# Spreading a bias copy over eight paced pieces, moving two weight loads, and adding a dummy square root in a one-core decoder layer

## What is computed

```python
h = rmsnorm(x, norm1_g[l])
cols = split_columns(h @ w_in[l])               # q, kc, vc, ks, vs, kw, vw, gates, c_q, c_kv, k_rope
o_nsa = nsa_mixer(..., t5_bias)                 # logits get t5_bias[t5_bucket(distance)]
o_mla = mla_mixer(c_q, c_kv, k_rope, positions, q_norm_g, w_q_up, kv_norm_g, w_kv_up)
x = x + concat(rmsnorm(o_nsa), rmsnorm(o_mla)) @ w_out[l]
x = x + peer_ffn(rmsnorm(x, norm2_g[l]), ...)
return rmsnorm(x, final_g)
```

## Time and profile before

| what | value |
|---|---|
| time, median of 3 runs | 1681.74 us (1678.98 to 1685.91) |
| the profiled execution | 1683.38 us, its span 1681.5 us |
| PE busy | 1614.3 us, 96% |
| DVE / ACT / POOL busy | 1311.4 / 661.5 / 358.1 us |
| mean granted clock of PE | 0.987 |
| chain that ended last | PE 51%, DVE 8%, DMA 8% |

### The profile page before, as it was taken

How to read it: one execution, slowest core, us unless ns; L and a number is a source line. 1 busy time by engine, 2 the same in 40 slices (tenths; PEclk the granted TensorE clock), 3 DMA queues, 4 the chain that set the end, 5 groups by cost and what they waited for, 6 DMA issues and landing times.

```text
span 1681.5 us, 25784 instructions
## 1 busy us (share of the span) xinstructions
PE 1614.3 (96%) x9131; PEld 1361.9 (81%) x9131; DVE 1311.4 (78%) x3054; ACT 661.5 (39%) x1037; POOL 358.1 (21%) x303
## 2 busy tenths in 40 slices
PE   7999999899999999998999999999999999999997
PEld 5877767788865678998999899997888887888885
DVE  3467777554668789998998888866888888888887
ACT  3345555432210233443544346653333333333333
POOL 1000020101000343232136550002222223222220
PEclk9999999999999999999999999999999999999999
DMA  7541000223236789887889995458999999999995
GB/s 256 165 139 37 2 2 2 83 84 125 75 94 226 227 299 311 281 286 260 266 275 348 343 331 193 127 158 292 315 324 332 320 321 342 326 318 326 318 331 203
DMA packets 198446, 380.78 MB, mean 226 GB/s; under 512 B 16291, under 2 KB 130787, under 8 KB 197708
## 3 DMA queue, kind: packets, MB, share of 16 engines
q1 hardware_dynamic: 159008, 226.39, 40.9%
q0 software_dynamic: 37952, 143.18, 24.4%
q10 hardware_dynamic: 1388, 9.98, 1.5%
HBM read 340.66 MB, written 41.98 MB: 228 GB/s over the span
## 4 chain that ended last, share of the span: by engine, by line
PE 51%; DVE 8%; DMA 8%; issue 2%; ACT 2%; SPq 0%; DVEq 0%; ACTq 0%
PE psum L2026 27%; PE psum L108 15%; PE psum L1775 7%; DMA v_first<-uT 4%; PE psum L1796 2%; DMA acts_in<-acts 2%; DMA u_raw<-uT 2%; DVE u_lo L1693 2%; DVE u_rows L1684 1%; ACT u_hi L1533 1%; DVE hot L1714 1%; DVE v_lo L1969 1%; DVE is L1708 1%; DVE x_back L1987 0%; DVE x_back L2016 0%
## 5 line engine op out<-in xcount | busy, mean ns | idle before, releaser
L108 PE MATMUL psum<-h_hi,u_hi 128*128 128x384 f32 x832 | 288.1, 346 | 19.8 <-DVE u_lo L1693 19.6
L2026 PE MATMUL psum<-v_hi,wa_hi 128*128 128x512 f32 x768 | 300.1, 391 | 6.3 <-DVE wa_lo L1976 4.4
L2026 PE MATMUL psum<-v_lo,wa_hi 128*128 128x512 f32 x768 | 299.6, 390 | 0.0
L2026 PE MATMUL psum<-v_hi,wa_lo 128*128 128x512 f32 x768 | 299.4, 390 | 0.0
L108 PE MATMUL psum<-h_lo,u_hi 128*128 128x384 f32 x832 | 280.7, 337 | 0.0
L108 PE MATMUL psum<-h_hi,u_lo 128*128 128x384 f32 x832 | 280.7, 337 | 0.0
L1524 POOL DMA_INDIRECT u_rows<-u,eid x128 | 190.8, 1490 | 342.4 <-DVE sdot L1684 301.6
L1937 ACT ACTIVATE v_hi<-v_raw 128x1024 fp32r<-128x1024 f32 x126 | 133.7, 1061 | 320.0 <-PE psum L2026 237.5
L1917 POOL DMA_INDIRECT v_rows<-v,eid x128 | 133.5, 1043 | 503.5 <-DVE x_back L1987 367.7
L1969 DVE TENSOR_TENSOR v_lo<-v_raw,v_hi 128x1024 fp32r<-128x1024 f32 x126 | 154.3, 1225 | 42.3 <-ACT v_hi L1937 41.1
L108 PEld LDWEIGHTS psum<-h_hi,u_hi 128*128 128x128 f32 x832 | 158.1, 190 | 24.7 <-DVE u_lo L1693 24.4
(11 more groups left out here) (317 smaller groups left out, 2664.5 us busy)
## 6 DMA issues: line engine op xcount, KB each, us to landing
v_raw<-v SPq DMA_DIRECT2D x126, 512.0 KB
u_raw<-uT SPq DMA_DIRECT2D x66, 512.0 KB
v_first<-uT SPq DMA_DIRECT2D x62, 512.0 KB
acts<-act_out SPq DMA_DIRECT2D x128, 192.0 KB
acts_in<-acts SPq DMA_DIRECT2D x128, 192.0 KB
wq_raw<-wq SPq DMA_DIRECT2D x16, 512.0 KB, 3.6
gates<-dense ACTq DMA_DIRECT2D x4, 2048.0 KB, 11.1
gates<-gates SPq DMA_DIRECT2D x31, 256.0 KB
```

The costliest lines, as they stand in the source:

```text
L108: mm = pe.matmul(bank, w[:, k, :], x[:, k, :], start=(i == 0), stop=(i == n - 1))
L2026: mm = pe.matmul(psum[:, 2 * t + b, :], w[:, c, ts], v[:, c, bs], start=(first and n == 0), stop=(last and n == 2), skip_group_check=True)
```

## The change

1. The copy of 4096 KB from `bias_rows` to `bias_rep` becomes eight DMAs of 512 KB, one for each head. They are issued behind the first four `pairs` copies, two at each count of `tile_mm` from 3 to 6. POOL waits for all eight ahead of the skewed load.
2. ScalarE's two loads of the up weights go from ahead of the first split to behind its split of tile 8 (`UP_AT = C0`, which is 8).
3. In `combine`, ScalarE waits for `fg`, takes a dummy square root (of zero times a column of `fg`) into a place that is written again later, and waits for it, ahead of the last norm.

```diff
             pool.wait_ge(b_out, 16)
-            pool.dma_start(io.bias_rep.rearrange("p (h n) -> p h n", h=HEADS),
-                           io.bias_rows.partition_broadcast(P)).then_inc(b_rep, 16)
-            pool.wait_ge(b_rep, 16)
...
                     pool.dma_start(pairs[DH:P, c, g, 0:S - 1], src[:, 1:S]).then_inc(pair_ok, 16)
+                if c == 0:
+                    rep = io.bias_rep.rearrange("p (h n) -> p h n", h=HEADS)
+                    rows = io.bias_rows.partition_broadcast(P)
+                    for h in range(HEADS):
+                        pool.wait_ge(tile_mm, R0 + 3 + h // 2)
+                        pool.dma_start(rep[:, h:h + 1, :], rows[:, h:h + 1, :]).then_inc(b_rep, 16)
+            pool.wait_ge(b_rep, 16 * HEADS)
             pool.dma_start(m.bias[:, :, :], skew).then_inc(b_tile, 16)
...
-            act.dma_start(m.wq_up[:, :, :], io.wq_up).then_inc(up_in, 16)
-            act.dma_start(m.wkv_up[:, :], io.wkv_up).then_inc(up_in, 16)
             split(0)
...
             for i in range(2, C0 + 2):
                 split(i)
+                if i == UP_AT:
+                    act.dma_start(m.wq_up[:, :, :], io.wq_up).then_inc(up_in, 16)
+                    act.dma_start(m.wkv_up[:, :], io.wkv_up).then_inc(up_in, 16)
...
+            act.wait_ge(fg_in, 16)
+            act.activation(stat[:, 2, QT - 1:QT], fg[:, 0:1], ACT.Sqrt, scale=0.0).then_inc(f_warm, 1)
+            act.wait_ge(f_warm, 1)
             for i, t in enumerate(order):
                 act.wait_ge(f_add, i + 1)
```

More of the change, by code:

```diff
@@ L191, in project @@
         UP_BANKS = 6
+        UP_AT = C0
         def is_row(i):
@@ L1863, in combine @@
         rest_in, fg_in = sem("rest_in"), sem("fg_in")
+        f_warm = sem("f_warm")
         block = ctx.enter_context(nc.Block())
```

## The result

| | before | changed |
|---|---|---|
| median of 12 runs each, us | 1679.89 (1676.3 to 1689.28) | 1674.41 (1665.6 to 1686.41) |
| ratio, 95% interval | 1 | 0.9952 (0.9931 to 0.9974) |
| span of the profiled execution, us | 1681.5 | 1673.1 |

The change makes the kernel 0.48% faster (0.26% to 0.69%), some 8 us by the ratio (5.5 by the medians), and the interval excludes that nothing changed. 1674.41 is 2.0 us above the predicted 1672.4, within its range of 1668.5 to 1678. Part of this closeness is luck: the kernel before has a median of 1679.89 us over twelve runs, where the forecast started from the 1681.74 of three. 9.4 us off 1679.89 would be 1670.5, and the measurement is 3.9 above that. The gain is just short of the bound of 0.5%, on the other side of which I had put 0.52 of the chance.

What follows compares the result with a forecast made beforehand. TensorE, busy for 96% of the span, was taken as the bound, with time to win only at its idle or low-clock places. 1683.38 - 8.27 - 1.10 = 1674.0 us profiled, so 1672.4 as median; range 1668.5 to 1678.

Steps and rivals of the forecast that it cites:

- the bound of 0.5%: Whole kernel: smallest difference a measurement can tell from no change, 8.4 us, that is 1673.3 us; chance of faster 0.52.
- The stall (part 1): Row tile 2 on PE: start comes 5.41 us forward and full clock returns 2.86 us, sum 8.27 us.
- the turns: DMA engines at the start: queues alternate one for one, 32 KB of copy per 2.7 KB of load, 2.0 us a turn.
- The loads beside the pieces: Row-tile loads during the paced copy: land in 5.6 us, within a slack of 8.6 us, so no cost.
- The up weights (part 2): Start and behind the split of tile 8: moving the two loads gains nothing and costs nothing.
- The end (part 3): Last norm in `combine`: the dummy brings square root's table load forward, gaining 1.10 us.
- The sum: Whole kernel: 8.27 and 1.10 us off the profiled execution; median 1672.4 us, 9.4 us (0.56%) less; chance 0.66.
- A: PE's later idle stretches: a lower clock answers one, or the 2.86 us is not returned; 1675.3 us; chance 0.12.
- B: Last norm: the dummy gives between -0.4 and +0.85 us; 1672.7 to 1673.9 us; chance 0.12.
- C: Row tiles: pieces starve their loads, 10.4 us for each stall; 1682.8 us with one, 1693 with two; chance 0.05.
- D: Row tile 2: full DMA engines, not the copy's packets, slow the load, so it still waits; 1676.5 us; chance 0.05.
- E: Whole kernel: the run's own spread may put a median 2 us to either side; lies over all, no separate chance.

Runs made afterwards that it cites:

- e1: Kernel before with only the copy in eight paced pieces, up weights at the start, no dummy; 1679.17 us in one execution.
- e6: Changed kernel with the copy as one DMA of 4096 KB issued at `tile_mm` 3; 1676.76 us in one execution.
- e4: Kernel before with the copy in eight 512 KB pieces, all issued at once at the old place, no dummy; 1672.13 us in one execution.
- e7: Changed kernel with the up weights loaded behind the split of column tile 10; ratio to the kernel before 0.9938 over 12 runs.
- e5: Changed kernel with the paced pieces cut by partitions, each 16 partitions with 32 KB rows; 1672.48 us in one execution.
- e8: Kernel before with the copy in two 2048 KB DMAs at once, rows of 16 KB, no dummy; 1671.73 us in one execution.
- e9: Kernel before with the copy in eight pieces at once at the old place, plus the dummy square root; ratio 0.9931 over 9 runs.
- e2: Kernel before with only the up-weight loads moved behind the split of tile 8, one copy as before; 1684.18 us in one execution.

## Why the prediction was right, and where it was not

**The stall (part 1): right, 8.27 us forecast, 8.3 measured.** e1 has 41.2 - 32.9. Both terms, the idle time and the low clock, are borne out: PE's granted clock is 1.00 throughout the stage, and e6 has brought both back.

**Why the load was slow: the turns are right, the place of the pacing was left open.** The prediction had it that small rows make the turns short, and added that by the rule of the Trainium skill (DMA: Bandwidth & Descriptors, Queues, rings and completion order) 4 KB rows would come in turns of 9 to 17 and only the pacing would help. e4 has no pacing and no stall, with about one packet for one in the queues, so the trace doesn't agree with that rule. The prediction had called the rule refuted before, and its reason was not enough: the copy has only eight packets an engine, so by the rule the load would have waited behind all of them, which also gives some 16 us. Only the packet counts and e4 decide it. Its turn of 16.1 / 8 = 2.0 us was also too long: a large packet takes 1.35, and the rest of the 16.1 is mostly the wait for the first packet.

**The loads beside the pieces: a little short.** 5.6 us were forecast from the 8.3 us of the earlier trace rows, which was the longer of two such loads (the next one beside `bias` landed in 5.9). Tile 6 to 8's landed in 5.1, 5.7 and 6.6, and tile 9's, 512 KB, in 8.0. They grow from tile to tile, as the backlog does: 341 GB/s asked for, and 302 to 309 carried from 35 to 50 us. All are under the slack, so PE didn't wait for a split.

**The up weights (part 2): the step that failed, by 0.4 us.** "Cost nothing" rested on the slack of a row tile's load against PE. It left out that ScalarE and VectorE must also copy the row products behind the split of tile 9, in the same short time. Tile 9's load met the last pieces and then the up weights, and PE waited for VectorE. e1 and e7, each without the up loads there, are 0.4 us quicker. But e5 has them at the same place and lost nothing: there tile 9's load landed in 6.5 us. So the up loads cost something only on top of the late pieces, and 0.4 us is the reading of one execution.

**The end (part 3): right.** 1.10 us forecast; the step from scaling to reciprocal went from 1.52 to 0.42, and the tail is 11.6 to 11.7 us in the five kernels without the dummy and 10.6 to 10.7 in the five with it. The table load did not wait for the gain, as the prediction had read from the earlier trace rows. The Trainium skill (ScalarE: Activation LUTs, What ACT_TABLE_LOAD costs) has 2.66 us for the switch with its drain; by the tail it is worth 1.0, and the measurement decides.

**The sum.** 8.3 + 1.1 - 0.4 = 9.0 us, against 9.4 forecast and some 8 measured with an interval from 4.4 to 11.6 (0.26% and 0.69% of 1679.89). The two profiled spans differ by 8.4, but this is partly chance. Tile 1 started 1.1 us later in the one of the changed kernel, which leaves 6.8 us at tile 9 and still 6.8 at the start of `experts`; `experts` then took 7.6 us less and `combine` 7.0 more, in code that is the same; the tail is 1.0 shorter. By the traces' clock records PE was at the low level for 13.7 us of `experts` before and 6.8 after, and for 3.4 and 10.2 us of `combine`. At half speed that is at most 3.4 us of each difference (an estimate); the rest is not explained.

**The rivals.** A (the clock takes it back) didn't happen in the stage touched: the clock is 1.00 there in all the kernels without a stall of several us. From tile 9 to `experts` it is low for 13.7 us both before and after, and that stretch takes 413.8 us in both. Behind that, the low stretches differ from execution to execution, and no run shows whether the change moves them. B's worst case is excluded by the 1.04 us that the Square has left. C's slack was right (8.7 us in e6) and its price per tile wrong: the copy is over after one stall, so the next load has nothing to share with. One such stall gives back the stage of before (41.0 us in e6), so C could hardly have made the kernel slower. D's forecast, that tile 2 still waits, is refuted by the changed kernel and e1, and its reason by e4, where the engines are full (share 1.03) and tile 2 doesn't wait. E is what decided between faster and same. The forecast was 1 us beyond the bound and the measurement 0.3 short of it; a chance of 0.52 for one side of it was as much as could be said.

## What to carry to other kernels

Here a DRAM copy with rows of 32 KB, and to a lesser degree one of 16 KB, slowed the small loads that shared the DMA engines with it, since the packets went about one for one. To look for this elsewhere, count the load's packets on an engine, multiply by the time of one packet of the copy, add the wait for the first packet (some 4 us here) and about 1 us for the landing, and compare the sum with the load's slack. For the kernel before this sum gives 10.8 + 4 + 1 = 15.8 us (16.1 measured); for e8 it gives 9.9, which is too little (12.3), so it is an estimate. Cutting the rows to 4 KB or pacing the copy each cured it, and cutting needs no new waits. A load that is moved into idle time of its issuing queue still has to be counted against every copy and split that falls due while it is in flight.

## What the runs showed of the hardware that I had not expected

- *A wait before the first turn.* With the copy queued ahead, 3.0 (e9) to 4.6 us (e2) pass before the load's first packet moves, with rows of 4, 16 or 32 KB alike, and 0.9 us with nothing beside it. Its cause stays open.
- *PE's start.* PE turns x at half its later rate at first: a transpose starts every 0.21 us, later every 0.11. The windows of the kernel before, then of the changed one, from 9 to 12 and 12 to 15 us (PE busy, then matmul records):

```profile
9.00:12.00 3.00, 3.00 (x12) 2.33 (x12) 2.08 (x6) 1.67 (x4) 0.63 (x1) 1.00 0.89 317
12.00:15.00 3.00, 3.00 (x27) 3.00 (x27) 1.00 (x4) 2.08 (x5) 0.67 (x2) 1.00 0.58 160
```

```profile
9.00:12.00 3.00, 3.00 (x14) 2.82 (x14) 1.86 (x6) 1.59 (x5) 0.73 (x1) 1.00 0.91 328
12.00:15.00 3.00, 3.00 (x16) 3.00 (x16) 2.20 (x5) 1.86 (x3) 0.00 (x0) 1.00 0.12 35
```

  The 1.00 in these windows is misleading. The trace's first record of the clock begins at 12.4 us in the one and at 15.2 in the other, just where the quick rate comes, and the view shows 1.00 where there is no record. The factor of two in the rate is that of the clock's two levels, so I read the slow start as the low level. The first record begins at 12.4 to 15.5 us in the ten executions and tile 1 starts at 24.1 to 25.7; the three with the earliest record have the three earliest tiles, and the one with the latest has the latest. With the up loads at the start tile 1 starts at 24.2 to 25.2, without them at 24.1 to 25.7. So the 1.1 us by which tile 1 was late in the changed kernel's profile go with the clock's rise, and these profiles show no effect of the change on it.
- *The length of an idle stretch does not tell whether the clock falls.* The stalls of 4.8 (e2), 5.3 (before) and 6.0 us (e6) were each followed by the low level, and in e8 two of 0.6 us were not. In between it goes both ways in one and the same trace. PE in the changed kernel, ahead of 1125 and of 1407 us, and the clock behind each:

```profile
1125.46 0.47 PE L2036 MATMUL psum<-v_hi,wa_hi 128*128 128x512 f32 x1 [1.94 <-PEq L1452]
1407.54 0.59 PE L2036 MATMUL psum<-v_hi,wa_hi 128*128 128x512 f32 x1 [1.80 <-DVE wa_lo L1986]
...
1126.00:1129.00 3.00, 3.00 (x15) 2.47 (x14) 1.70 (x3) 0.77 (x2) 0.51 (x1) 1.00 0.16 54
1408.00:1411.00 3.00, 3.00 (x9) 2.33 (x8) 3.00 (x6) 0.52 (x1) 1.08 (x1) 0.50 0.95 293
```

  1.94 us of idle time left it at 1.00, and 1.80 us was followed by 0.50. What else decides was not tried.
